# Mixer products with an operand in PSUM, level 0 of the inverse first, and a recurrent tail one iteration later

## Time and profile before

| | |
|---|---|
| median of 3 runs | 3606.62 us (3606.58 to 3607.71) |
| the profiled execution | 3606.58 us, its span 3604.8 us |
| PE busy | 3310.2 us (92%) |
| DVE busy | 2144.2 us (59%) |
| ACT, POOL busy | 1563.0 us (43%), 1772.4 us (49%) |
| phase one, two | about 952 us, 577 us |

### The profile page before, as it was taken

How to read it: one execution, slowest core, us unless ns; L and a number is a source line. 1 busy time by engine, 2 the same in 40 slices (tenths; PEclk the granted TensorE clock), 3 DMA queues, 4 the chain that set the end, 5 groups by cost and what they waited for, 6 DMA issues and landing times.

```text
span 3604.8 us, 60424 instructions
## 1 busy us (share of the span) xinstructions
PE 3310.2 (92%) x21604; PEld 2986.8 (83%) x21604; DVE 2144.2 (59%) x3370; ACT 1563.0 (43%) x2196; POOL 1772.4 (49%) x2328
## 2 busy tenths in 40 slices
PE   5999999999989999999997987989888899999998
PEld 4898999899877888888874977888887688888886
DVE  5777767776745763763774656666665543434343
ACT  4344443443334443443434554444453443434343
POOL 2545554555434554554532434555553354545553
PEclk7999999999989999999999998999999999999999
DMA  4655666565565555655543746655655555555553
GB/s 157 208 190 193 205 194 198 184 213 180 176 238 173 187 181 183 187 180 186 183 150 129 268 156 215 208 174 180 207 186 210 182 186 187 184 186 184 185 186 111
DMA packets 262396, 673.03 MB, mean 187 GB/s; under 512 B 28263, under 2 KB 66888, under 8 KB 261448
## 3 DMA queue, kind: packets, MB, share of 16 engines
q1 hardware_dynamic: 262152, 669.81, 56.8%
HBM read 663.38 MB, written 6.32 MB: 186 GB/s over the span
## 4 chain that ended last, share of the span: by engine, by line
PE 71%; DVE 15%; issue 4%; ACT 4%; DMA 3%; SPq 1%; POOL 0%; DVEq 0%; ACTq 0%
PE psum L642 26%; PE psum L643 13%; PE psum L635 6%; PE psum L637 6%; PE psum L636 6%; PE psum L640 2%; PE psum L712 2%; DVE psum L478 1%; PE psum L1409 1%; DMA ada_raw<-w_ada 1%; PE psum L1418 1%; DVE work L766 1%; DVE work L1265 1%; DMA work<-w_ada 1%; PE psum L1416 1%
## 5 line engine op out<-in xcount | busy, mean ns | idle before, releaser
L500 POOL TENSOR_TENSOR w_lo<-raw,w_hi 128x256 fp32r<-128x256 f32 (+1 forms) x2324 | 1772.2, 793 | 1802.9 <-ACT w_hi L487 1802.6
L487 ACT ACTIVATE w_hi<-raw 128x1024 fp32r<-128x1024 f32 (+3 forms) x1112 | 1050.1, 948 | 1420.1 <-PE psum L637 618.3
L635 PE MATMUL psum<-act_a,w_lo 128*128 128x256 f32 x3072 | 922.3, 300 | 33.3 <-DVE w_lo L500 12.4
L500 DVE TENSOR_TENSOR w_lo<-raw,w_hi 128x1024 fp32r<-128x1024 f32 (+3 forms) x444 | 529.8, 1193 | 629.2 <-ACT w_hi L487 621.6
L636 PE MATMUL psum<-act_a,w_hi 128*128 128x256 f32 x3072 | 886.5, 289 | 0.0
L637 PE MATMUL psum<-act_a,w_hi 128*128 128x256 f32 x3072 | 886.4, 289 | 0.0
L642 PE MATMUL psum<-act_a,w_hi 128*128 128x512 f32 x2295 | 828.4, 403 | 27.4 <-DVE act_a L754 10.6
L642 PE MATMUL psum<-act_b,w_hi 128*128 128x512 f32 x2096 | 755.0, 402 | 18.7 <-DVE act_b L1652 9.7
L643 PE MATMUL psum<-act_a,w_lo 128*128 128x256 f32 x2295 | 647.8, 282 | 0.0
L635 PEld LDWEIGHTS psum<-act_a,w_lo 128*128 128x128 f32 x3072 | 607.3, 198 | 43.6 <-issue 19.4
L636 PEld LDWEIGHTS psum<-act_a,w_hi 128*128 128x128 f32 x3072 | 607.2, 198 | 3.1 <-issue 1.9
(11 more groups left out here) (335 smaller groups left out, 3124.2 us busy)
## 6 DMA issues: line engine op xcount, KB each, us to landing
raw<-w_mlp SPq DMA_DIRECT2D x256, 512.0 KB, 4.2
raw<-w_up SPq DMA_DIRECT2D x176, 512.0 KB, 3.7
raw<-w_dil SPq DMA_DIRECT2D x192, 384.0 KB, 3.5
work<-w_ada SPq DMA_DIRECT2D x288, 256.0 KB, 3.9
raw<-w_hg SPq DMA_DIRECT2D x128, 320.0 KB, 3.2
raw<-w_delta SPq DMA_DIRECT2D x64, 512.0 KB, 3.9
raw<-w_out SPq DMA_DIRECT2D x64, 512.0 KB, 6.0
raw<-w_down SPq DMA_DIRECT2D x64, 512.0 KB, 4.2
```

What stands on the lines that cost most here:

```text
L487: act.activation(w_hi[:, t % SPLIT, 0:nb * P], raw[:, t % RAW, 0:nb * P], ACT.Copy)\
L500: ins = eng.tensor_tensor(w_lo[:, t % SPLIT, cols], raw[:, t % RAW, cols], w_hi[:, t % SPLIT, cols], ALU.subtract)
L635: pe.matmul(bank[:, 0:S], wl, src[:, kt, 0:S], start=first, stop=False)
```

## The change

- **An operand or the result in PSUM.** DVE instructions of the mixers that read two SBUF tiles now mostly read one from PSUM: the accumulators of both convolutions, the Newton step (three instructions in place of four, signs and factors moved into the later constants), scaled k and q, q times decay, three of HGRN's four products, the log gate that is scanned, hyena's spectrum products and last product. To this end ACT writes PSUM: the centre tap of the delta convolution as a second copy out of each projection tile (`delta_tiles_act`), the centre taps of hyena's, three of the exponentials, the log gate.
- **Level 0 first.** The products of the decays with the Gram matrix of k come first, then level 0 and `delta_z0`, and a hop later the products for q.
- **Turned forms.** In levels 1 to 5, Y^T Z is no longer computed. X alone is updated; PE transposes X in the next level, and ACT copies that to Z. A dilated-attention step negates the scores so that a minimum serves as the exponential's bias.
- **HGRN earlier, its tail later.** HGRN's steps start at item 10 and not 13, with v's transposes at item 14, scores at item 18 as before, updates at 20 and outputs at 22. Its norm and gate run in the next pass's items 0 to 5, ahead of hyena in each hop. Hyena's convolution is spread over items 1 to 3, and u's transposes move from item 4 to 5. One more pass of phase two is written out.
- **Small.** ACT does the copies of per-head parameters and HGRN's k factor, which DVE did.

The diff, cut to its core:

```diff
+                        if late and ph.turn:
+                            one(at, at // 2, at % 2, False, False)
+                            ph.was_late, at = True, at + 1
...
+        def newton(ch, dve, v, y, p, out, scale, bias):
+
+            ch.step(dve.scalar_tensor_tensor(p, v, bias / scale, y, ALU.add, ALU.mult))
             ch.settle()
-            ch.step(dve.scalar_tensor_tensor(t, v, bias / scale, t, ALU.add, ALU.mult))
+            ch.step(dve.tensor_tensor(p, p, y, ALU.mult))
             ch.settle()
-            ch.step(dve.tensor_scalar(t, t, -0.5 * scale, 1.5, ALU.mult, ALU.add))
-            ch.settle()
-            ch.step(dve.tensor_tensor(t, t, y, ALU.mult))
+            ch.step(dve.scalar_tensor_tensor(out, p, 3.0 / scale, y, ALU.subtract, ALU.mult))
             ch.settle()
...
+                wait(act, "item_used", ph.tile_done(i, k))
+                wait(act, "rule_hi", i + 1)
+                wait(act, "delta_conv", i * 3 + k)
+                if k == 0:
+                    wait(act, "dil_vT_out", i)
+                a = acc[:, ph.bank(k), 0:S]
+                act.activation(d_t[:, k, 2:S + 2], a, ACT.Copy)
+                act.activation(conv_place, a, ACT.Copy, scale=d_hp[:, 5 * k + 2:5 * k + 3])\
+                   .then_inc(sem("tile_out"), 1)
...
+                wait(act, "delta_ax", i * 12 + 1)
+                act.activation(d_x, A2(mix[:, 4, :], a=4), ACT.Copy).then_inc(sem("delta_x_out"), 1)
+                yield
+                for s in range(2, 7):
+                    yield
+                    yield
+                    wait(act, "delta_ax", i * 12 + (2 * s - 1))
+                    act.activation(d_z, A2(mix[:, 4, :], a=4), ACT.Copy).then_inc(sem("delta_x_out"), 1)
+                yield
+                yield
...
+                        ins = dve.scalar_tensor_tensor(d_c[:, c, :] if j == 4 else conv_place,
+                                                       d_t[:, c, j:j + S],
+                                                       d_hp[:, 5 * c + j:5 * c + j + 1], conv_place,
                                                        ALU.mult, ALU.add)
-                        if c < 2 or j < 4:
+                        if j < 4:
                             ch.step(ins)
-                    if c < 2:
-                        yield
+                            ch.settle()
...
+                newton(ch, dve, t, d_kq, A2(mix[:, 1, :], a=2), t, 1.0, EPS)
...
+                def gammas(kind):
+                    g = mix[:, 2, :].rearrange("p (k c j) -> p k c j", k=2, c=2)[:, :, kind, :]
+                    for d in range(2):
+                        ins = dve.tensor_tensor(A2(d_bq[:, d, kind, :], a=2),
+                                                A2(d_e[:, d, kind, :], a=2), g, ALU.mult)
+                    return ins
+                ch.step(gammas(0))
+                ch.settle()
+                for k in range(2):
+                    ins = dve.tensor_tensor(A2(mix[:, 3, :], a=4)[:, k::2, :],
+                                            d_bq[:, :, 0, k * P:(k + 1) * P],
+                                            bc(lev[:, 0:P], 2), ALU.mult)
+                ch.step(ins)
+                ch.settle()
+                dve.tensor_tensor(d_z, bc(ident, 4), A2(mix[:, 3, :], a=4), ALU.subtract)\
+                   .then_inc(sem("delta_z0"), 1)
+                yield
+                gammas(1)
+                wait(dve, "delta_gamma", i * 2 + 2)
                 wait(dve, "delta_kq", i + 1)
                 for d in range(2):
                     k = SECOND[d]
                     ins = dve.tensor_tensor(d_qd[:, d, :], d_kq[:, 1, k * P:(k + 1) * P],
-                                            d_wn[:, d, :], ALU.mult)
+                                            mix[:, 0, d * P:(d + 1) * P], ALU.mult)
...
                     dve.tensor_tensor(d_y, A2(mix[:, 2, :], a=4), bc(lev[:, s * P:(s + 1) * P], 4),
                                       ALU.mult).then_inc(sem("delta_y"), 1)
                     yield
                     wait(dve, "delta_xy", i * 6 + s)
-                    ins = dve.tensor_tensor(d_z, d_z, A2(mix[:, 4, :], a=4), ALU.subtract)
                     if s < 6:
                         ins = dve.tensor_tensor(d_x, d_x, A2(mix[:, 3, :], a=4), ALU.subtract)
+                    else:
+                        ins = dve.tensor_tensor(d_z, d_z, A2(mix[:, 4, :], a=4), ALU.subtract)
                     ins.then_inc(sem("delta_level"), 1)
                     yield
                 wait(dve, "delta_first", i + 1)
@@ -1347,19 +1380,19 @@
                 yield
...
                 for s in range(1, 7):
                     if s == 1:
-                        wait(pe, "delta_x_out", i + 1)
+                        wait(pe, "delta_x_out", i * 6 + 1)
+                        wait(pe, "delta_bq", i + 1)
                     else:
                         wait(pe, "delta_level", i * 6 + (s - 1))
+                        for m in range(4):
+                            ins = pe.transpose(mix[:, 4, m * P:(m + 1) * P], d_x[:, m, :], ident)
+                        ins.then_inc(sem("delta_ax"), 1)
...
                     wait(pe, "delta_y", i * 6 + s)
+                    wait(pe, "delta_x_out", i * 6 + s)
                     for m in range(4):
                         if s < 6:
-                            pe.matmul(mix[:, 3, m * P:(m + 1) * P], d_z[:, m, :], d_y[:, m, :],
-                                      start=True, stop=True)
-                        ins = pe.matmul(mix[:, 4, m * P:(m + 1) * P], d_y[:, m, :], d_z[:, m, :],
-                                        start=True, stop=True)
+                            ins = pe.matmul(mix[:, 3, m * P:(m + 1) * P], d_z[:, m, :], d_y[:, m, :],
+                                            start=True, stop=True)
+                        else:
+                            ins = pe.matmul(mix[:, 4, m * P:(m + 1) * P], d_y[:, m, :], d_z[:, m, :],
+                                            start=True, stop=True)
                     ins.then_inc(sem("delta_xy"), 1)
                     yield
...
+                act.wait_ge(sem("hgrn_tanh"), i + LATER)
+                for d in range(2):
+                    act.activation(h_lf[:, d, :], h_th[:, d, :], ACT.Ln,
+                                   scale=h_p[:, d, 0:1], bias=h_p[:, d, 1:2])
+                    ins = act.activation(h_kk[:, d, :], h_th[:, d, :], ACT.Identity,
+                                         scale=h_p[:, d, 2:3], bias=h_p[:, d, 0:1])
+                ins.then_inc(sem("hgrn_log"), 1)
+                yield
+                yield
+                yield
+                wait(act, "hg_exponents", i + 1)
+                act.activation(A2(mix[:, 1, :], a=2), h_d, ACT.Exp)
+                act.activation(A2(mix[:, 2, :], a=2), h_d, ACT.Exp, scale=-1.0)
+                act.activation(A2(mix[:, 3, :], a=2), h_e3, ACT.Exp)
+                act.activation(h_e4, h_a, ACT.Exp).then_inc(sem("hg_decays"), 1)
+                for _ in range(5):
+                    yield
+                wait(act, "hgrn_kT", i + LATER)
+                act.activation(h_kT, A2(mix[:, 2, :], a=4), ACT.Copy).then_inc(sem("hgrn_kT_out"), 1)
...
                                                 a, ALU.subtract)
...
+                    dve.tensor_tensor(h_e1, A2(mix[:, 1, :], a=2), q, ALU.mult)
+                    yield
+                    dve.tensor_tensor(h_e2, A2(mix[:, 2, :], a=2), h_kk, ALU.mult)
+                    dve.tensor_tensor(h_e3, A2(mix[:, 3, :], a=2), h_kk, ALU.mult).then_inc(sem("hg_products"), 1)
+                    yield
+                    ch.step(dve.tensor_tensor(h_qa, h_e4, q, ALU.mult))
...
+                def tail(i):
+                    ct.begin(dve, i)
+                    yield
                     wait(dve, "rule_gtanh", i + LATER)
-                    ch.step(dve.scalar_tensor_tensor(h_o[:, 1, :], h_o[:, 1, :], 1.0, h_z[:, 4, :],
+                    ct.step(dve.scalar_tensor_tensor(h_o[:, 1, :], mix[:, 2, 0:S], 1.0, h_z[:, 4, :],
                                                      ALU.add, ALU.mult))
-                    yield
...
+                for c in range(3):
+                    ins = act.activation(y_c[c], y_t[:, c, :], ACT.Identity,
+                                         scale=y_hp[:, 3 * c + 1:3 * c + 2],
+                                         bias=y_hp[:, 9 + c:10 + c])
+                ins.then_inc(sem("hy_middle"), 1)
+                for _ in range(12):
...
         def two_mixers(who, eng, hyena, hgrn):
             ph = PHD["two"]
-            return [(0, 13, 1, hyena(eng), -1), (18, 3, 1, ada_finish(who, eng, ph), 0),
-                    (13, 11, 1, lambda i: hgrn(ph.late)(i), 0)]
+            main, tail = hgrn
+            return [(0, 6, 1, lambda i: tail(ph.was_late)(i), -1), (0, 14, 1, hyena(eng), -1),
+                    (18, 3, 1, ada_finish(who, eng, ph), 0),
```

(28 more changed lines are left out.)

377 lines of the change are left out of this document (171 added, 206 removed).

## The result

The changed kernel takes **3492.5 us** (median of 4 runs, 3489.8 to 3499.8) against 3606.6 for the kernel before on the same chip (3604.3 to 3607.7): ratio 0.969, 95% interval 0.967 to 0.970. The gain is 114 us where 136 were forecast; the time lies in the range. The profiled execution took 3489.75 us, its span is 3488.0.

What follows compares the result with a forecast made beforehand. TensorE, busy 92%, was taken to lose time waiting for VectorE's late queue in the mixers and at half clock. Phase one 70 us (8.7 a pass) plus phase two 66 make 136, from 3606.6 to 3470 us; range 3430 to 3530.

Steps and rivals of the forecast that it cites:

- Newton step and scaled k, q: Phase one, VectorE: 5.6 us becomes 3.1 with three instructions of 0.69 us and two of 0.42; saves 2.5 a pass.
- Start at the guess: Phase one: the Newton step begins when ScalarE's guess is there, at 214.1 not 215.1, as earlier taps get faster; 1.0 us.
- Level 0 first, 1.7: Phase one: half of L1307 (0.7) and L1313 (1.0) go behind `delta_z0`, saving 1.7 us; mask products stay at 1.69 for two.
- Turned forms, 2.0: Phase one, inverse levels: half of the second hop's 1.71 us less 0.45 for transposes, five times; 2.0 us of TensorE's time.
- Clock, 1.5 of 2.0: Phase one: of the 2.0 us a pass lost to half clock after L1399, 1.5 taken as saved, ends 0 and 2.0.
- TensorE's wait for that w_lo: Phase two, item 18: ScalarE waits for VectorE's differences, then four exponentials, with splits behind; TensorE waits 1.4 us, ends 0 and 3.
- both falls go: Phase two: with no wait above 1.4 us both clock falls vanish, 3.2 us a pass, of which 3.0 is taken.
- Hyena's wait: Phase two, before hyena's transposes: PSUM operands and ScalarE's centre taps leave 0.3 us of wait in place of 2.6.
- the waits shrink but the clock still falls: Rival, 19%: phase one keeps 3.5 us and half clock, phase two 3.8 us and one fall; 5.2 saved a pass each, 3526.
- The rival in which all waits go: Rival, 14%: mask products run at 0.42 us each and POOL is in time, so all waits go; 3440 us.
- The rival that the PSUM operands are no faster: Rival, 4%: only the order saves, 1.7 + 2.0 us a pass in phase one and 3 in phase two; 3552 us.
- The rival of the slower kernel: Rival, 4%: ScalarE becomes the engine waited for; sign turns at 8.5 us of new waits a pass, at 10 us 3630.

Runs made afterwards that it cites:

- the SBUF variant: The changed kernel with the running sum of the twelve delta convolution taps in SBUF instead of PSUM: 3492.1 us, ratio 0.969 to the kernel before.
- the small kernel: Separate kernel timing VectorE's 128x256 instructions by operand place, GpSimd idle, then subtracting: two SBUF sources 419 ns alone, 0.93 us beside it; one PSUM source 417 and 415 ns.

## Why the prediction came out as it did

**Phase one: 71 us measured, 70 forecast, from terms that were off and made up for each other.** That the sum is right to 1 us is in part luck. Per pass:
- *Newton step and scaled k, q: saves 2.5.* Measured 2.7 (5.6 to 2.9). Right; the variant with it undone gives 2.2 of it back (5.1 us in its fifth pass).
- *Start at the guess, 1.0.* Only 0.5: an accumulation that began at 203.15, just before the guess (203.22), keeps VectorE until 203.82. The taps before it are worth nothing, as the SBUF variant showed.
- *Level 0 first, 1.7, mask products left at 1.69.* The chain behind the scaled q is only 1.1 us shorter: 1.7 from the order, 0.9 from the mask products that I had left to a rival, less 1.4 for the differences. I hadn't foreseen that these could grow. Saved in the chain are thus 4.3 us and not 5.2, which leaves a wait of about 2.4 and not 1.6; it is 2.9, and the last 0.5 us isn't accounted for.
- *Turned forms, 2.0.* Measured 2.5, in the trace and by undoing them (20 us). The first hop got 0.44 us longer (0.81 to 1.25), as forecast; the second lost 0.90 and not half of 1.71. Five times that is 2.3; the other 0.2 is the first hop of level 1, which ran partly at a lower clock before (0.59 from 235.0 to 235.5; 1.01 us, now 0.83).
- *Clock, 1.5 of 2.0.* About 1.9: TensorE's busy time in phase one fell by 35 us, of which the turned forms are 20. The 2.0 was 5 us times the 40% by which 21 matmuls in 4 us fall short of 35.
- *In sum:* 36 us of waits (42 forecast; L1387, 5.2 us, was counted, L1574, 2.7 us, was not), 20 us of forms (16) and 15 us of clock (12).

**Phase two: 45 us measured, 66 forecast. Two terms failed.** TensorE's waits there fell by 32 us where 42 were forecast, its busy time by 13 where 24 were.
- *"I put TensorE's wait for that w_lo at 1.4 us, ends 0 and 3."* The mechanism was right, in place and order; the size was 2.4 us. 8 us in all. The step that I had named but not priced is ScalarE's wait of 2.2 us for the differences, which take 0.72 to 0.96 us each beside GpSimd.
- *"With no wait above 1.4 us both falls go."* With 2.4 us one of them stays: TensorE's busy time fell by 1.6 us a pass (60.6 to 59.0), not by 3.0. 11 us in all.
- Hyena's wait went to nothing, as forecast, but I counted its gain eight times where the last pass has none (2.3 us). The growth at the very end, 2.7 forecast, was 3.3. Against that, the 0.3 us that I left in the other seven passes went too (2.1 us), and the new wait before hyena's transforms (2.8 us more) is balanced by 2.8 us less before v's transposes. These small terms leave about 1 us, and with the 8 and 11 us above they make the gap of 21 within rounding.

The exponentials moved by one item give 21 us, which shows the first two (it also took what I had left standing, 1.4 us a pass). The first half of the phase's gain, that the wait for the scores would go, came true, but no run shows by which part of the change; my reading of the start as the bound of that chain is refuted.

Of the rivals, "the waits shrink but the clock still falls" has phase two nearly right: it keeps 3.8 us of waits and one fall, 39 us with the end, against 45 measured. For phase one it gives 42, against 71.

Of the signs, three were missed: the wait of L1432 (2.9 us, 1 to 2 named), that for the low half of item 18 (2.4, 1 to 2 named), and the clock, which is 1.00 in three of seven stretches from wait to wait in phase one and in one of seven in phase two.

**The PSUM operand.** The prediction said that the duration goes by the operands. It goes by the operands *and* by what GpSimd does at the same moment: in the small kernel 928 ns with two SBUF sources beside GpSimd, 419 with GpSimd idle, 415 with a PSUM source beside it. The first pair of rows that I set against each other (0.69 us at 229.49 and 1.22 at L2014) can't show the operands at all: both instructions read two SBUF tiles (the first the identity and its own), and they differ in that GpSimd's burst was over beside the first (at 229.18) and running beside the second. The rival in which all waits go had said that the slow instructions depend on what runs beside them; that reading was the right one. The mask products got faster by their new place alone, the differences slower by theirs. The rival that the PSUM operands are no faster was wrong on the path; delta's taps are faster with it too (0.49 us, 0.84 in SBUF), but that is worth nothing in the time. The rival of the slower kernel had its mechanism right (the exponentials wait at item 14 and the split stands behind), but its size, 2.4 us a pass, is far from the 8.5 at which it would decide the sign.

## What to carry to other kernels

Before you price a VectorE instruction by a row of the same shape, look at what GpSimd does during that row and during the place where the instruction will stand: two SBUF sources of 128x256 cost 0.42 us with GpSimd idle and 0.93 beside its subtractions. Give a PSUM source first to those that stand in a chain beside GpSimd's work; with one of the two in PSUM it was 415 ns there, while a PSUM result doesn't help (933 ns, 928 with an SBUF result). And where an in-order engine both feeds the matmuls and serves a chain, put the feeding step ahead of the chain's wait: one position gave 3.1 us a pass, half of it through the clock.

## What was not expected of the hardware

- A scaling of one SBUF tile (128x256) went by every 0.21 us with GpSimd idle and every 0.72 beside it (8 in 1.7 and 5.8 us): with one SBUF source it loses by the largest factor.
- VectorE lost more than GpSimd: 0.34 to 0.86 us from start to start for two SBUF sources, while GpSimd's block went from 0.66 to 0.80.
- The clock doesn't go by the length of the wait alone. Of the eight waits before level 0 in the changed kernel, those of 2.80, 2.79 and 2.63 us were followed by granted clock 1.00, those of 2.71, 2.80 and 2.72 us by 0.59, 0.69 and 0.70, and the two of 3.2 us by 0.50 and 0.52. Two of these stretches stand below, second and fourth pass, each after a wait of 2.80. Why they differ isn't settled here. After the wait before item 18 (2.4 to 2.5 us in all eight passes) it was 0.50 to 0.70 in six of them and 1.00 in the first and the last.

```profile
216.00:219.00 3.00, 3.00 (x27) 3.00 (x27) 2.35 (x7) 1.49 (x3) 1.61 (x3) 1.00 0.95 320
...
430.50:433.50 3.00, 3.00 (x20) 3.00 (x20) 1.77 (x6) 1.52 (x3) 0.35 (x1) 0.69 0.90 323
```
